# Two attention layers: probabilities stay unnormalised, and transposed reciprocals of their sums are multiplied in afterwards

## The reference, cut to what matters

```python
# second layer (moba_mixer; 256 tokens are one block, so it is causal attention)
p = masked_softmax(s_own, m_own).astype(v.dtype)      # e / max(sum(e), 1e-30)
o = jnp.einsum('bcgrk,bkgd->bcgrd', p, v_own)
y = (o * jax.nn.silu(z)) @ w_out

# third layer: heads 0 to 7 with a sink and a bias, heads 8 to 15 with a bias
p = jax.nn.softmax(jnp.concatenate([s, sink_col], axis=-1), axis=-1)[..., :span]
o_a = jnp.einsum('bgrqk,bkgd->bqgrd', p, vb)
...
mixed = jnp.concatenate([rms_norm_2(o_a, out_norm_a[layer]), rms_norm_2(o_b, out_norm_b[layer])], axis=-1)
x = x + gate1[:, None, :] * (mixed @ w_out[layer])
```

## Time and profile before

| | us |
|---|---|
| median of 3 runs | 1343.13 |
| lowest and highest run | 1341.51 to 1344.74 |
| profiled execution: span on the engines | 1340.0 |
| median less that span | 3.1 |
| attention and first projection of the second layer, first score to tile 1's projection | 308.83 to 346.27 |
| the same of the third layer | 423.45 to 475.50 |

### The profile page before, as it was taken

How to read it: one execution, slowest core, us unless ns; L and a number is a source line. 1 busy time by engine, 2 the same in 40 slices (tenths; PEclk the granted TensorE clock), 3 DMA queues, 4 the chain that set the end, 5 groups by cost and what they waited for, 6 DMA issues and landing times.

```text
span 1340.0 us, 21959 instructions
## 1 busy us (share of the span) xinstructions
PE 1266.5 (95%) x8283; PEld 1098.2 (82%) x8283; DVE 1063.1 (79%) x2318; ACT 597.1 (45%) x1105; POOL 252.1 (19%) x180
## 2 busy tenths in 40 slices
PE   5988899988999899999989999999999999999997
PEld 5577865676697569999979999999988888888886
DVE  5587896787677688999998888899977777777776
ACT  1434683536243525565544444444443433333332
POOL 0354000460000005699950000000000000000001
PEclk9999999999999999999999999999999999999999
DMA  9877632857578335454434444444465555555553
GB/s 355 288 236 265 239 131 64 299 211 260 188 276 303 110 134 213 158 196 164 172 127 158 146 154 149 151 158 144 156 214 194 190 196 196 189 195 197 189 194 105
DMA packets 92382, 256.82 MB, mean 192 GB/s; under 512 B 9472, under 2 KB 16896, under 8 KB 91904
## 3 DMA queue, kind: packets, MB, share of 16 engines
q1 hardware_dynamic: 59728, 195.91, 41.9%
q10 hardware_dynamic: 32560, 59.66, 12.4%
HBM read 254.47 MB, written 1.06 MB: 191 GB/s over the span
## 4 chain that ended last, share of the span: by engine, by line
PE 57%; DVE 26%; DMA 5%; POOL 4%; issue 4%; ACT 3%; SPq 1%; ACTq 0%; DVEq 0%; POOLq 0%
PE bank L1736 25%; PE bank L1729 17%; PE bank L2008 4%; PE bank L1123 3%; DVE arena L434 2%; PE bank L693 2%; DVE arena L970 2%; DMA arena<-in_w_in 2%; POOL head_ms L824 2%; DVE arena L1833 1%; DVE arena L1828 1%; DMA arena<-in_nsa_w_in 1%; DVE u_lo L685 1%; DVE arena L1933 1%; DVE v_lo L685 1%
## 5 line engine op out<-in xcount | busy, mean ns | idle before, releaser
L1729 PE MATMUL bank<-h_hi,u_hi 128*128 128x256 f32 x632 | 180.8, 286 | 5.1 <-POOL u_lo L1768 4.0
L1729 PE MATMUL bank<-h_lo,u_hi 128*128 128x256 f32 x632 | 176.4, 279 | 0.0
L1729 PE MATMUL bank<-h_hi,u_lo 128*128 128x256 f32 x632 | 176.4, 279 | 0.0
L1729 PEld LDWEIGHTS bank<-h_hi,u_hi 128*128 128x128 f32 x632 | 119.0, 188 | 6.5 <-POOL u_lo L1768 2.8
L2165 POOL TENSOR_SCALAR raw<-raw 128x1024 f32<-128x1024 f32 x1 | 3.4, 3435 | 627.2 <-DMA raw<-in_final_g 627.2
L1729 PEld LDWEIGHTS bank<-h_hi,u_lo 128*128 128x128 f32 x632 | 119.5, 189 | 0.0
L1729 PEld LDWEIGHTS bank<-h_lo,u_hi 128*128 128x128 f32 x632 | 119.3, 189 | 0.0
L2104 ACT ACTIVATE u_hi<-raw 128x1024 fp32r<-128x1024 f32 x64 | 68.0, 1062 | 104.3 <-PE bank L1736 104.3
L2104 ACT ACTIVATE v_hi<-raw 128x1024 fp32r<-128x1024 f32 x64 | 68.0, 1062 | 101.1 <-PE bank L1736 101.1
L1729 PE MATMUL bank<-h_hi,v_hi 128*128 128x256 f32 x392 | 111.3, 284 | 0.9 <-POOL v_lo L1768 0.9
L1729 PE MATMUL bank<-h_lo,v_hi 128*128 128x256 f32 x392 | 109.2, 279 | 0.0
(11 more groups left out here) (275 smaller groups left out, 3471.3 us busy)
## 6 DMA issues: line engine op xcount, KB each, us to landing
raw<-in_u SPq DMA_DIRECT2D x128, 512.0 KB, 3.5
raw<-in_v SPq DMA_DIRECT2D x128, 512.0 KB, 3.5
arena<-in_ada_t SPq DMA_DIRECT2D x80, 512.0 KB, 4.9
arena<-in_ada_w SPq DMA_DIRECT2D x12, 512.0 KB, 12.1
raw<-in_nsa_w_in ACTq DMA_DIRECT2D x3, 2048.0 KB, 12.0
arena<-in_moba_w_in ACTq DMA_DIRECT2D x3, 2048.0 KB, 14.9
arena<-in_w_in ACTq DMA_DIRECT2D x3, 2048.0 KB, 10.2
arena<-in_w_query ACTq DMA_DIRECT2D x3, 2048.0 KB, 10.9
```

The lines of the kernel that those rows point to most:

```text
L1729: last = pe.matmul(zbank[k].t[:, 0:S], u[:, c, :], h[:, c, :], start=n == 0, stop=n == 3 * DC - 1)
```

## The change

For the second and third layer `normalise` is no longer issued. The exponentials are transposed as they are. `reciprocals` adds the sink's term, takes the reciprocal of the sums and writes it 64 times over (once for each feature of a head), capped at 1e30, into a buffer `widened`. `spread` transposes that buffer into bank 5, and `weigh` multiplies it into silu(z) (second layer) or with the norm's weights into `hT` (third layer). `done` then multiplies the outputs with that.

```diff
+        def reciprocals(p):
+
+            t, _, lo, hi, _ = pairs[p]
+            rs = rsum[:, t, lo:hi]
+            V.need(m_ex[p])
+            if sink is not None and hi <= sink.shape[1]:
+                V.need(V.did(ve.tensor_tensor(rs, rs, esink[:, t, lo:hi], ALU.add)))
+            V.need(V.did(ve.reciprocal(rs, rs)))
+            V.need(spread_read[0], *widened[1])
+            m_rec[p] = V.did(ve.tensor_scalar(widened[0][:, 0:hi - lo, :], rs.unsqueeze(2).broadcast_to([P, hi - lo, HD]), 1e30, None,
+                                              ALU.min))
+
+        def spread(p):
+
+            t, _, lo, hi, _ = pairs[p]
+            b = banks[5]
+            T.need(b.free, m_rec[p])
+            for i in range((hi - lo) // 2):
+                last = pe.transpose(b.t[:, i * P:(i + 1) * P], widened[0][:, 2 * i:2 * i + 2, :].rearrange("p h d -> p (h d)"), ident[:])
+            spread_read[0] = m = T.did(last)
+            V.need(m)
+            b.free = weigh(t, lo // 2, hi // 2, b.t[:, 0:(hi - lo) // 2 * P].rearrange("p (c q) -> p c q", q=P))
...
-                T.need(b.free, m_nm[p, par])
+                T.need(b.free, m_nm[p, par] if weigh is None else m_exp[p, par])
...
+                if weigh is not None:
+                    V.need(banks[5].free)
                 banks[6].free, banks[7].free = done(t, m)
...
-            if 0 <= p - 1 < n:
-                normalise(p - 1)
+            if weigh is None:
+                if 0 <= p - 1 < n:
+                    normalise(p - 1)
+            else:
+                if 0 <= p - 2 < n:
+                    spread(p - 2)
+                if 0 <= p - 1 < n:
+                    reciprocals(p - 1)
...
+        def weigh_z(t, lo, hi, spread_out):
+            part = zT[:, lo:hi, t * P:(t + 1) * P]
+            V.need(m_z)
+            return V.did(ve.tensor_tensor(part, spread_out, part, ALU.mult))
...
+        def weigh_norm(t, lo, hi, spread_out):
+            return V.did(ve.tensor_tensor(hT[:, lo:hi, t * P:(t + 1) * P], spread_out,
+                                          norm_cols[:, lo:hi].unsqueeze(2).broadcast_to([P, hi - lo, P]), ALU.mult))
...
-                for c in range(4):
-                    mv = V.did(ve.tensor_scalar(hT[:, 4 * half + c, t * P:(t + 1) * P], bank[:, c, :],
-                                                norm_cols[:, 4 * half + c:4 * half + c + 1], None, ALU.mult))
-                banks[6 + half].free = mv
+                part = hT[:, cs, t * P:(t + 1) * P]
+                banks[6 + half].free = V.did(ve.tensor_tensor(part, bank, part, ALU.mult))
...
-                for half in range(2):
-                    for c in range(4):
-                        last = pe.matmul(b.t[:, half:half + 1], squares[:, 4 * half + c, :], ones[:, 0:1], start=c == 0,
-                                         stop=c == 3)
+                for c in range(DC):
+                    last = pe.matmul(b.t[:, 2 * c:2 * c + 2], squares[:, c, :], half_of_p, start=True, stop=True)
                 squares_read[0] = T.did(last)
-                V.need(squares_read[0])
-                b.free = V.did(ve.tensor_scalar(rstds[:, t, :], b.t[:, 0:2], 1.0 / (HA * HD), EPS, ALU.mult, ALU.add))
+                V.need(squares_read[0], m_rr)
+                b.free = V.did(ve.tensor_tensor(head_squares[:, t, :], b.t[:, 0:NH], rsum_squared[:, t, :], ALU.mult))
+                V.need(b.free)
+                V.need(V.did(ve.tensor_reduce(rstds[:, t, :], head_squares[:, t, :].rearrange("p (a h) -> p a h", a=2), AX, ALU.add)))
+                b.free = V.did(ve.tensor_scalar(rstds[:, t, :], rstds[:, t, :], 1.0 / (HA * HD), EPS, ALU.mult, ALU.add))
```

More of the change, by code:

```diff
@@ L930, in add_outputs, with attend @@
         return inst
-    def attend(branches, q_of, bias_of, first_of, causal_keys, marks, v_marks, begin, done, tail, loads, fills, sink=None):
+    def attend(branches, q_of, bias_of, first_of, causal_keys, marks, v_marks, begin, done, tail, loads, fills, sink=None,
+               weigh=None, widened=None):
         spare_pair[0] = 4
@@ L940, in attend @@
         n = len(pairs)
-        m_sc, m_ex, m_nm, m_cp = {}, {}, {}, {}
+        m_sc, m_ex, m_nm, m_cp, m_exp, m_rec = {}, {}, {}, {}, {}, {}
+        spread_read = [None]
         def heads(p, par):
@@ L979, in exponentials @@
                                                   accum_out=rsum[:, t, h:h + 1]))
+                m_exp[p, par] = m_ex[p]
             if sunk:
@@ L1565, in build @@
         tail, rest = gated_out(moba_out0, moba_out1, 1, [b[1] for b in bufs])
+        m_z = A.last()
+        def weigh_z(t, lo, hi, spread_out):
+            part = zT[:, lo:hi, t * P:(t + 1) * P]
+            V.need(m_z)
+            return V.did(ve.tensor_tensor(part, spread_out, part, ALU.mult))
         attend([(lambda h, w: kT[half_of(h), h // GQA, 0:w],
@@ L1568, in build @@
                lambda h, t: qT[half_of(h), h // 2, t * P:(t + 1) * P],
-               causal_bias, lambda h: 3e38, True, [copied["q"], copied["k"]], [copied["v"]], lambda t: None, times_z(zT), tail, (qa, biases), (1, 3, 1))
+               causal_bias, lambda h: 3e38, True, [copied["q"], copied["k"]], [copied["v"]], lambda t: None, times_z(zT), tail, (qa, biases), (1, 3, 1),
+               weigh=weigh_z, widened=(bufs[0][0][:, 0:8 * HD].rearrange("p (h d) -> p h d", d=HD), all_last()))
         first_norm, factors, turn_first, place_first, finish = modulated(2, col("norm1_g_2"), 0, 8)
@@ L1624, in build @@
         V.need(m_ns)
+        half_of_p = carve([P, 2], s2)
+        m_halves = V.did(ve.tensor_reduce(half_of_p, ident[:].rearrange("p (a n) -> p a n", a=2), AX, ALU.add))
         m_ready = [V.last(), A.last()]
@@ L1640, in build @@
         rstds = carve([P, NT, 2], s2)
+        widened = carve([P, 4, HD], s2)
+        head_squares = carve([P, NT, NH], s2)
+        rsum_squared = carve([P, NT, NH], s2)
         squares_read = [None]
+        def weigh_norm(t, lo, hi, spread_out):
+            return V.did(ve.tensor_tensor(hT[:, lo:hi, t * P:(t + 1) * P], spread_out,
+                                          norm_cols[:, lo:hi].unsqueeze(2).broadcast_to([P, hi - lo, P]), ALU.mult))
         def normed(t, m):
+            m_rr = V.did(ve.tensor_tensor(rsum_squared[:, t, :], rsum[:, t, :], rsum[:, t, :], ALU.mult))
             A.need(m, squares_read[0])
@@ L1658, in sum_squares @@
                 fill_wait(1, b)
-                T.need(b.free, m_s, m_ones)
-                for half in range(2):
-                    for c in range(4):
-                        last = pe.matmul(b.t[:, half:half + 1], squares[:, 4 * half + c, :], ones[:, 0:1], start=c == 0,
-                                         stop=c == 3)
-                squares_read[0] = T.did(last)
-                V.need(squares_read[0])
-                b.free = V.did(ve.tensor_scalar(rstds[:, t, :], b.t[:, 0:2], 1.0 / (HA * HD), EPS, ALU.mult, ALU.add))
+                T.need(b.free, m_s, m_halves)
+                for c in range(DC):
+                    last = pe.matmul(b.t[:, 2 * c:2 * c + 2], squares[:, c, :], half_of_p, start=True, stop=True)
+                squares_read[0] = T.did(last)
+                V.need(squares_read[0], m_rr)
[3 more added lines that the diff above has]
+                b.free = V.did(ve.tensor_scalar(rstds[:, t, :], rstds[:, t, :], 1.0 / (HA * HD), EPS, ALU.mult, ALU.add))
                 G.need(b.free, m_pow)
@@ L1680, in build @@
                bias_of, lambda h: nsink[:, h:h + 1] if h < HA else 3e38, False, [*m_ready, *biases.marks], [m_vb], lambda t: None,
-               normed, tail, (query0,), (2, 5, 1), sink=row("sink_a_2"))
+               normed, tail, (query0,), (2, 5, 1), sink=row("sink_a_2"),
+               weigh=weigh_norm, widened=(widened, []))
         run_later(True)
```

## The result

| | us |
|---|---|
| before, median of 4 runs (lowest to highest) | 1343.53 (1341.51 to 1344.74) |
| after, median of 4 runs (lowest to highest) | 1350.76 (1345.92 to 1352.48) |
| ratio, 95% interval | 1.0049 (1.0029 to 1.0070) |
| span of the profiled execution, before and after | 1340.0 and 1344.6 |
| the changed kernel timed again, 6 runs, beside 29 runs of before | 1348.74 and 1343.94, ratio 1.0041 (1.0027 to 1.0055) |

The change makes the kernel slower, by 7.2 us in the first measurement and by 4.8 in the second. The profiled execution of the changed kernel took 1345.92 in all, 1.3 over its span. With 1.3 for before too, its profiled execution took about 1341.3, 2 us under the median (an estimate).

The account below looks back on a forecast made before the run. VectorE was taken to bound the attention bodies before, the ring of TensorE's waits after; 1.1 + 1.1 + 0.3 + 1.1 + 0.4 = 4.0 us made the span 1344.0 and the median 1347.1, range 1343.2 to 1349.6 (8 in 10).

Parts of the forecast that it names:

- Ring: Both attention bodies: TensorE's spread, scores, outputs, transposes and ScalarE's two copies set the pace, 4.16 us a pair, 4.42 with 8 heads.
- Second layer's body: Second layer's attention up to tile 0's projection: the projection starts at 336.5 instead of 335.40, +1.1 us.
- Tails: End of tile 0 in both layers: the last spread stands ahead of the projection's second half, +1.1 us each.
- Third layer's body: Third layer's attention up to tile 0's projection: the projection starts at 461.1 against 460.79, +0.3 us.
- The end of the third layer: Release of the bank L191 waits for: three small instructions depend on one another, two more at 0.2, +0.4 us.
- near twice as large: VectorE's work in both layers: counted in columns alone, the relief would be near twice the 5.6 to 7.9 us.
- The clock: Two named 1.2 GHz stretches of before: changed kernel put at 2.4 GHz there; a fall on its chain costs about 1.
- the rival with further falls: Same waits, and the clock falls on the chain once or twice more: 1348.3 us, chance 0.15.
- around the span: Outside the profiled span: median less span, 1343.13 - 1340.0 = 3.1 us, added to the forecast span.
- Shorter rings: Both bodies: each ring 0.25 us shorter over eight rings, 2.0 less, giving 1345.1 us; chance 0.25.
- VectorE keeps the pace and the relief comes through: Bodies of attention: VectorE stays the pace, 3.3 us less, 1339.8; chance 0.08.
- Waits covered: Spread's transposes do not hold up TensorE's queue, all tails covered: 1343 us; chance 0.02.

Follow-up runs that it names:

- wait_only: The kernel before plus dummy transposes into bank 5 at spread's place in both layers, waiting for ScalarE's copy, computing nothing used: 1350.28 us, ratio 1.0055 to before.
- late_spread: The changed kernel with every spread and the reciprocals issued later, behind scores and the half projection, directly ahead of outputs: ratio 0.9975 to before.
- layer2_only: The changed kernel with the third layer kept as before, so only the second layer is changed: ratio 1.0015 to before.
- widen_twice: The changed kernel with the widening instruction issued twice, 4.3 us more work for VectorE: ratio 1.0040 to before.
- same_before: The kernel before run once more without any edit, 12 runs: ratio 0.9992, from 1340.14 to 1345.62 us.
- same_after: The changed kernel run once more without any edit, 6 runs: 1348.74 us, ratio 1.0041 to before.
- fill_first: The changed kernel with five dummy products ahead of the second layer's first spread alone: ratio 1.0022 to before.
- late_bank4: The changed kernel with spread and reciprocals issued later, ahead of outputs, and spread's transposes put in bank 4 instead of 5: 1338.22 us, ratio 0.9954 to before.

## Why the prediction was right, and where it failed

The direction and the mechanism of the waits were right. The time was not: 1350.76 us lies above the stated range, and the step that failed is the one on the clock.

**The waits: right, by place and nearly by size.** `spread` waits for ScalarE's second copy in every pair. Ring 4.50 in the second layer (predicted 4.42) and 4.28 in the third (4.16). That these waits are the loss is shown by `wait_only` (alone they cost as much) and by `late_spread` (covered, the loss turns into a gain). The reading of the third layer before was wrong in one point that changed no term: its chain does not alternate between L978 and L1651, which are single pieces of 2.1 and 2.2 us, but runs on VectorE (L970, L434 and L1010) from 423.56 to 444.31 but for short gaps, as in the second layer.

**The terms of the sum**, first profile against first profile. Second layer's body +1.1, measured 28.06 - 26.57 = 1.49. Tails +1.1 each, 1.19 and 1.18. Third layer's body +0.3, measured 38.75 - 37.41 = 1.34: mis-sized, since the sums of squares of tile 0 hold up VectorE through L1717 and L1719, which I counted for the end of the layer alone. Against `layer2_only`, whose third layer is as before and has no fall, it is even 38.75 - 36.46 = 2.29. The end of the third layer +0.4: from the second half to tile 1 it is 54.09 - 38.75 - 5.68 = 9.66 against 52.05 - 37.41 - 4.50 = 10.14, but before had a fall in it; against `layer2_only` without one, 50.21 - 36.46 - 4.51 = 9.24, it is +0.42. In all 2.67 + 2.04 = 4.71 for 4.0. That the spans differ by 4.6 is partly luck: ahead of the second layer's first score the changed kernel's profile is 0.47 us shorter, between the two attentions 0.79 shorter, and behind them 1.15 longer. The first score alone comes between 306.35 and 309.20 us over all the profiles.

**VectorE: right.** Busy 1063.1 before and 1056.3 after, 6.8 less, for 5.6 to 7.9. The widening took 294 ns, the lower of its bounds (428 at 512 columns, which I had doubled); weighing 423, but 692 and not 640 at 512 columns. From 256 to 512 columns widening grows by 428 - 294 = 134 ns and weighing by 692 - 423 = 269, twice as much. That agrees with the tier table of the Trainium skill (VectorE: DVE Perf Modes, "The perf-mode tier table"), which has 32-bit tensor_scalar in SBUF at twice the rate of tensor_tensor, out of PSUM too. It matters little here, as `widen_twice` shows: VectorE has slack. The prediction's "near twice as large" does not come out: it takes away 16384 columns and adds 10240, and the difference at the 1.26 ns a column of what it takes away, with 0.9 us for the small instructions, would be 8.6 us.

**The step that failed: "The clock".** I put the changed kernel at 2.4 GHz and gave the rival with further falls 0.15, because "no idle time is as long as before". The order says otherwise: with `scores` behind `spread`, TensorE has nothing left between the first transposes and the first copy, and idles 2.82 us, where before it idled at most 0.83 in one piece near that place and 1.75 in the whole of both attentions. In four profiles of five with this gap a fall followed, 1.6 us on the chain (29.66 for 28.06), where I had priced a fall at about 1; the fall at the end of the third layer puts tile 1 another 1.1 later (55.22 for 54.09). The two are 2.7 of the 2.9 us between the two profiles of the changed kernel. The same step hid a second error: it named two falls of the kernel before, overlooked a third (474 to 477 us), and left all three in the times that the sum starts from. Those in the third layer cost 52.05 - 50.21 = 1.8 us, the one in the second about 1.5, so the sum took them for the kernel's own pace. The first profile after, with none, flatters the change. Read with falls as most profiles have them, the second layer's tile 1 comes at 41.7 instead of 37.5 and the third's at 55 instead of 52. That is 7 us against the profile of before, as much as the first measurement moved, and the median of the second moves by 5. The 2 us between are what the profile of before lies under its own median. Where in the program they arise is not shown; a stretch at the lower clock at 680 to 690 us is in some profiles of either kernel (in `same_before` and `after`, not in `before` or `same_after`). That the falls carry the median out of the range is therefore argued from single profiles; the one experiment on it, `fill_first`, leaves the gain between nothing and 3 us.

**The range** was bounded by costs alone and had no room for the runs: the same before ran from 1337.77 to 1348.41, and a median of four runs of the changed kernel (1350.76) lies 2.0 above one of six (1348.74). My 3.1 us "around the span" was not a constant either: it is 1.3, and the rest was a profiled execution faster than the median.

**The rivals.** Shorter rings: no, they are 0.1 longer than their parts. The clock falls on the chain once or twice more: this is the nearest, with 1348.3 beside 1348.74 and 1350.76. VectorE keeps the pace and the relief comes through: not here, but with the waits covered a gain of that size came (`late_bank4`, 5.4 us; leaving out the multiplications brought 5.3). Waits covered: only after moving them. Of the signs named, L1034 waits for L1048 in every pair, 0.74 us in the tails, and VectorE's products wait for L1034; TensorE's wait for the multiplications is gone (before, it idled 6.1 us for L1010 and 1.1 for L1006 ahead of L1019).

## What to carry to other kernels

An instruction put into an in-order queue costs what its wait holds up behind it, not what it takes: ahead of the same 32 transposes TensorE idled for 13.8 us in one place and for 2.4 in another, where work that needed nothing stood in front. So when a bank is reused, issue the reuse behind the independent work; that the bank that comes free first is the better one is likely from the waits (2.4 for 4.1 us) but not clear of the noise in time. And before pricing against one profile, mark which stretches of it ran at the lower clock, since the change can move them.

## What the runs showed of the hardware

A gap of 2.82 us in TensorE's work was followed within 1 us by 3.4 us at 1.2 GHz in four of five profiles that had it, and not in the fifth (`after`); what decides is not shown. The same place in the same instructions had a fall in one profile (`before`, around an idle time of 1.46 us) and none in another (`layer2_only`, 1.45). One dummy product of 0.43 us in each gap did not stop it; with five in the one long gap the one profile taken had none. A VectorE instruction that reads each number 64 times over took 294 ns for 256 columns, against 13.7/48 = 285 in a row (mean of one 349) for one that reads each once.
